# Two recurrent blocks run side by side and earlier, other column orders, and half-width first levels, in a two-model Trainium2 kernel

## The chip, the cores and the metric

The kernel runs on one core of one Trainium2 chip. A core has a matrix engine (TensorE, PE in the profile), a vector engine (VectorE, DVE), an engine for functions such as exp (ScalarE, ACT), a general one (GpSimd, POOL) and one that mostly issues transfers (SyncE, SP). PE writes its results to PSUM, which has 8 banks; everything else lies in SBUF. The metric is the device time of one launch in microseconds, median of several runs.

## The reference, cut to what matters

Two models run after each other: two transformer layers, and then two layers of a hybrid. Each hybrid layer is a *mixer* followed by a feed-forward part. The change touches the mixer alone, which runs twice. T is 528 tokens.

```python
proj = jnp.einsum('btd,dc->btc', h, w_in)
hq, hf, hi, hg, rq, rk, rv, rg, lx, ly = jnp.split(proj, IN_SPLITS, axis=-1)
... # HGRN: 4 heads of width 128, from hf (decay, key), hq (query), hi (value)
o_hg = merge_heads(rmsnorm(o_hg, hg_norm_g)) * jax.nn.silu(hg)
... # retention: 4 heads, from rq, rk (with rope) and rv
o_ret = merge_heads(head_groupnorm(o_ret, ret_norm_g)) * jax.nn.silu(rg)
xc = causal_dwconv(lx, lru_conv_w, lru_conv_b)          # 4 taps, 256 channels
o_lru = rg_lru(xc, gate_a_w, gate_a_b, gate_i_w, gate_i_b, lru_lambda) * jax.nn.gelu(ly)
merged = jnp.concatenate([o_hg, o_ret, o_lru], axis=-1)
return jnp.einsum('btc,cd->btd', merged, w_out)

# rg_lru: r and i are sigmoids of two block-diagonal products of xc
log_a = -LRU_C * r * softplus(-lam);  a = exp(log_a)
u = sqrt(-expm1(2.0 * log_a)) * (i * x);  h_t = a_t h_{t-1} + u_t
```

## The kernel before, in words

**Matrix products.** A weight tile of 128 columns is brought from memory to `raw` by SP, copied to a rounded high part `WH` by ACT (`highs`, L1207) and subtracted to a low part `WL` by DVE (`lows`, L1761). Each product is made of three PE passes (low weights, low activations, both high; `part`, L516). The high part of unit u+3 can be made when PE has finished unit u, so `highs` for it stands in ACT's program right behind the eviction of unit u; DVE's `lows` stands two slots later in its own program. Every engine runs its program strictly in order.

**The mixer.** PE computes the columns of `w_in` tile by tile in the order of `MIXER_TILES`; GH and GL are the high and low part of the merged result, whose 8 blocks (0 to 3 HGRN heads, 4 and 5 retention, 6 and 7 LRU) are read by the output projection in `out_first`. A plain tile has 8 *slots* (one for each of 8 contraction steps, 6 matmuls of 264 columns each), a wide one (`v0`, `v1`, `rv`: values, computed by `wide_tokens`, L604) has 20. Slots are counted through: `lx0` is slots 1 to 8, `lx1` 9 to 16, `v0` 17 to 36, `hf1` 37 to 44, `hq1` 45 to 52, `hg1` 53 to 60, `rq0` 61 to 68, up to slot 196, and the output projection's first two tiles bring slots 197 to 208.

**The woven work.** HGRN's heads, LRU, retention and the two gates are generators, one for each engine. `Threads` advances them: a work `(generator, n, a, b)` makes its step i at slot a + ceil(i (b-a) / n). So head 0 `(14, 1, 52)` makes step 6 at slot 20, 7 at 27 and so on by the same rule on PE, ACT and DVE; the step's work is put into the engine's program behind that slot's. Slots order the programs, they don't synchronise the engines: an engine waits only where an instruction waits on a semaphore. ACT evicts a tile after the steps of that tile's last slot; in the wide tile it evicts bank by bank, the last bank after the steps of the last slot.

**An HGRN head.** Step 1 on DVE makes the decay A (L2209) and the key K (`hK`, L2211) and prepares level 0. Steps 2 to 7 are the levels -1 to 4: PE multiplies 32-column blocks (L967) into bank 4, DVE merges the bank under a mask (`merge`, L2203) and prepares the level after next (`prep`, L2186 to L2199). PE's next level may write bank 4 only after the merge before it. Step 8 is levels 5 and 6, step 9 transposes (L993), step 10 PE makes the chunk states (L1001, L1003, which read the values `VI` of the wide tile) and DVE chains them, step 11 PE makes the head's output (L1019) and ACT squares and copies it (L1543, L1544), step 12 PE sums the squares, ACT makes the inverse root (a table load and `Ln` and `Exp`, L1547 to L1550) and DVE scales (L2251), step 13 DVE gates (L2256) and ACT copies to GH (L1553), step 14 DVE makes GL (L2259).

**LRU, block n of 2.** Each block runs alone, through one set of buffers (`xc`, `la`, `li`, `tmp[3]`), so block 1 begins after block 0's scan. `(lru(), 8, 10, 60)` gives slots 17, 23, 29, 35 for block 0 and 42, 48, 54, 60 for block 1. The four steps: DVE's convolution (L2273, L2276); PE's product for gate a (L523) and ACT's sigmoid (L1564); PE's product for gate i, ACT's sigmoid, tanh and exp (L1567, L1569, L1570), DVE's products (L2281 to L2286); ACT's square root (L1573), DVE's product and scan (L2289, L2291).

**Retention's norm.** At slots 176 and 180 PE makes the means, at 184 and 187 the variances (L523), both into banks 6 and 7; ACT takes `Ln` and `Exp` of each (L1608, L1610).

**The ends.** `lru_gate` (slots 176, 180, 184) multiplies by gelu(ly) and writes blocks 6 and 7; `ret_gate` (194, 200, 206) writes blocks 4 and 5. `out_first` reads the blocks in the order 0, 1, 2, 6, 7, 3 in its first two tiles, and `finish_tile` adds 4 and 5.

Of the kernel before, what the change touches and what calls it, by code (L numbers as in the profile page):

```python
# [8 lines left out]
T = 528  # L9
# [262 lines left out]
def build(nc, wts, xT, mT, pp, cst, cstm, tA, tR, causal, biasT, gates, out, spill):  # L272
# [10 lines left out]
    with ctx:  # L283
# [87 lines left out]
        at = Counts()  # L371
# [127 lines left out]
        def pe_program(nc, e):  # L499
# [531 lines left out]

            def lru(l):
                for n in range(2):
                    yield
                    pe.wait_ge(*at("lconv", l, n))
                    pe.wait_ge(gw_loaded, 16 * (l + 1))
                    take(6, 7)
                    ones_sum(gw[:, n, :], xc, two(3), True, True).then_inc(*pe.up("lga", l, n))
                    give((6, 7), ("lsa", l, n))
                    yield  # L1040
                    take(6, 7)
                    ones_sum(gw[:, 2 + n, :], xc, two(3), True, True).then_inc(*pe.up("lgi", l, n))
                    give((6, 7), ("lsi", l, n))
                    yield
                    yield

# [34 lines left out]
            def ret_values(l):  # L1081
# [36 lines left out]
                for n in range(2):  # L1118
# [17 lines left out]
            def mixer(l, between):  # L1136
# [19 lines left out]
                UO = first[f"mo{l}"]  # L1156
                out_first(UO, works, GH, GL, (0, 1, 2, 6, 7, 3), [pair_of(0, ver), pair_of(1, ver)], ("gl", l), 0)

                def tiles(m, r):
                    if m < 2:  # L1160
                        finish_tile(UO + m, r, GH, GL, (4, 5), ("gl", l), 0)
                    else:
                        tile(UO + m, r, GH, GL)
# [30 lines left out]
        def act_program(nc, e):  # L1194
# [361 lines left out]
            def lru(l):  # L1556
                lbv = lbvs[l]
                for n in range(2):
                    yield
                    act.wait_ge(*at("lga", l, n))  # L1560
                    if n:
                        act.wait_ge(*at("la6", l, 0))
                    act.wait_ge(*at("dk", l, 25))
                    nc.scalar.activation(la, pair_bank(3), ACT.Sigmoid, bias=par("gab", 2 * l + n)).then_inc(*act.up("lsa", l, n))  # L1564
                    yield
                    act.wait_ge(*at("lgi", l, n))
                    nc.scalar.activation(li, pair_bank(3), ACT.Sigmoid, bias=par("gib", 2 * l + n)).then_inc(*act.up("lsi", l, n))  # L1567
                    act.wait_ge(*at("lsa", l, n))
                    nc.scalar.activation(tmp[3], la, ACT.Tanh, scale=lbv[:, 24 + n:25 + n]).then_inc(*act.up("lth", l, n))  # L1569
                    nc.scalar.activation(la, la, ACT.Exp, scale=lbv[:, 26 + n:27 + n]).then_inc(*act.up("lea", l, n))  # L1570
                    yield
                    act.wait_ge(*at("la3", l, n))
                    nc.scalar.activation(tmp[3], tmp[3], ACT.Sqrt).then_inc(*act.up("lsq", l, n))  # L1573
                    yield

# [15 lines left out]
            def ret_values(l):  # L1591
# [12 lines left out]
                for n in range(2):  # L1604
                    act.wait_ge(*at("rvar", l, n))
                    act.wait_ge(*at("hst", l, 3, 3))
                    nc.scalar.preload_act_table_set("natural_log_exp_and_others")
                    nc.scalar.activation(tmp_rs[n][:, :], pair_bank(3), ACT.Ln, bias=eps6).then_inc(*act.up("rl", l, n))  # L1608
# [11 lines left out]
            def mixer(l):  # L1620
# [129 lines left out]
        def dve_program(nc, e):  # L1750
# [416 lines left out]
            def hgrn(l, h):  # L2167
# [3 lines left out]
                def prep(lev):  # L2171
# [11 lines left out]
                    if lev:  # L2183
                        dve.wait_ge(*at("hA", l, h, lev - 1))
                    if lev < 2:
                        nc.vector.tensor_tensor(qa[:, :], Q[:, :], A[:, :], ALU.mult).then_inc(*dve.up("hd1" if lev else "hp", l, h, lev))  # L2186
                    else:
                        nc.vector.tensor_tensor(QAv[:, :, 1, :], Qv[:, :, 1, :], Av[:, :, 1, :], ALU.mult).then_inc(*dve.up("hd1", l, h, lev))
# [73 lines left out]
            def lru(l):  # L2262
                for n in range(2):
                    x = LX[n]
# [6 lines left out]
                    if n:  # L2271
                        dve.wait_ge(*at("la6", l, 0))
                    nc.vector.tensor_scalar(xc, x[:, 3:T + 3], cw(3), par("lcb", 2 * l + n), ALU.mult, ALU.add).then_inc(*dve.up("lc", l, n, 0))  # L2273
                    for j in range(3):
                        dve.wait_ge(*at("lc", l, n, j))
                        nc.vector.scalar_tensor_tensor(xc, x[:, j:j + T], cw(j), xc, ALU.mult, ALU.add  # L2276
                                                       ).then_inc(*dve.up(*(("lc", l, n, j + 1) if j < 2 else ("lconv", l, n))))
                    yield
                    yield
                    dve.wait_ge(*at("lsi", l, n))  # L2280
                    nc.vector.tensor_tensor(xc, xc, li, ALU.mult).then_inc(*dve.up("lix", l, n))  # L2281
                    dve.wait_ge(*at("lea", l, n))
                    dve.wait_ge(*at("lix", l, n))
                    nc.vector.tensor_tensor(li, la, la, ALU.mult).then_inc(*dve.up("la2", l, n))
                    dve.wait_ge(*at("la2", l, n))
                    nc.vector.scalar_tensor_tensor(tmp[3], li, 1.0, tmp[3], ALU.add, ALU.mult).then_inc(*dve.up("la3", l, n))  # L2286
                    yield
                    dve.wait_ge(*at("lsq", l, n))
                    nc.vector.tensor_tensor(xc, xc, tmp[3], ALU.mult).then_inc(*dve.up("la5", l, n))  # L2289
                    dve.wait_ge(*at("la5", l, n))  # L2290
                    nc.vector.tensor_tensor_scan(hseq[n], la, xc, 0.0, ALU.mult, ALU.add).then_inc(*dve.up("la6", l, n))  # L2291
                    yield

# [18 lines left out]
            def ret_scores(l):  # L2312
                for n, r in enumerate((RQ, RK)):
                    dve.wait_ge(*at("rperm", l, n))
                    dve.wait_ge(tab_loaded, 16 * (l + 1))
                    dve.wait_ge(*(at("la6", l, 1) if n else at("lconv", l, 1)))
                    nc.vector.tensor_tensor(rraw[n], rraw[n], tab[:, 2 * n, :], ALU.mult).then_inc(*dve.up("rropec", l, n))
# [278 lines left out]
```

## Time and profile before

| what | value |
|---|---|
| median of 3 runs | 2693.39 us (2691.96 to 2695.31) |
| the profiled execution | 2695.57 us, its span 2693.8 us |
| PE / DVE / ACT busy | 2609.5 / 1367.1 / 1058.2 us (97% / 51% / 39%) |
| first mixer, slots 1 to 196 | 1357.6 to 1578.2 us of the span |
| second mixer, slots 1 to 196 | 2035.7 to 2255.0 us |

Times of the trace are microseconds from the first instruction. In a waits view a row says which engine and line waited for which, then the sum, the number of waits and the longest. In a timeline a row has the start, the duration, engine, line, operation, operands and count, and in brackets the idle time before it with what ended it. `ACT_TABLE_LOAD` is ACT's change from one set of functions to another. In a row of a windows view stand the stretch and its length, the busy time of PE, PE's weight loads, DVE, ACT and POOL with the number of instructions, the granted TensorE clock as a share of full speed (1.00 is the 2.4 GHz level, 0.50 the 1.2 GHz level), the DMA engines' busy share and GB/s.

### The profile page before, as it was taken

Reading aid. Unit: us, or ns where it says so; the run is one execution under the profiler, and the core shown is the slowest. Engines: PE = TensorE matmul, PEld = TensorE weight load, DVE = VectorE, ACT = ScalarE, POOL = GpSimd, SP = SyncE. Lnnn points to the kernel's source line nnn. Section 1 sums busy time; section 2 is a strip of 40 time slices with the busy share of each in tenths; the row PEclk is TensorE's granted clock in tenths of the full one; section 3 lists DMA queues with packets and bytes.
Section 4 is the critical chain, followed back from the end, with each engine's and each line's share of the span. In section 5 each row is a group of like instructions: output and inputs, shape, how many; then the busy total and the mean of one; then the engine's idle time right before and its main releaser. Section 6 shows DMA issues by size and latency. Waiting matters only on the chain.

```text
span 2693.8 us, 42806 instructions
## 1 busy us (share of the span) xinstructions
PE 2609.5 (97%) x18948; PEld 2327.8 (86%) x18948; DVE 1367.1 (51%) x2195; ACT 1058.2 (39%) x1713; POOL 30.6 (1%) x69
## 2 busy tenths in 40 slices
PE   7999999999999999999999999999999999999998
PEld 5776888888877788888798899999999889999998
DVE  4776633324555653332566546555336654655533
ACT  3554422222444442221454344444225444444421
POOL 0000000000000000000000000000000000000000
PEclk9999999999999999999999999999999999999999
DMA  4221122222222122232221222222223122222222
GB/s 164 83 87 62 67 97 98 95 87 90 94 79 79 64 78 94 94 102 88 81 98 48 84 91 79 95 91 80 99 87 123 48 84 80 90 95 94 90 87 75
DMA packets 39467, 236.04 MB, mean 88 GB/s; under 512 B 5248, under 2 KB 7296, under 8 KB 17008
## 3 DMA queue, kind: packets, MB, share of 16 engines
q1 hardware_dynamic: 34336, 213.93, 23.5%
q0 software_dynamic: 3792, 17.26, 1.8%
q8 instruction: 149, 2.44, 0.4%
q10 hardware_dynamic: 1152, 2.10, 0.2%
q14 instruction: 38, 0.31, 0.0%
HBM read 222.65 MB, written 6.42 MB: 85 GB/s over the span
## 4 chain that ended last, share of the span: by engine, by line
PE 85%; DVE 8%; ACT 6%; DMA 1%; issue 0%; ACTq 0%; DVEq 0%
PE P L516 72%; PE P L626 2%; PE P L604 2%; PE P L523 2%; DVE WL L1761 2%; ACT WH L1207 1%; PE P L881 1%; PE P L638 1%; PE P L652 1%; PE P L681 1%; PE P L967 1%; DVE X L2061 1%; DVE small L2064 1%; DMA X<-in_xT 0%; PE P L857 0%
## 5 line engine op out<-in xcount | busy, mean ns | idle before, releaser
L516 PE MATMUL P<-XH,WL 128*128 128x264 f32 (+3 forms) x3080 | 850.2, 325 | 35.0 <-DVE WL L1761 19.4
L516 PE MATMUL P<-XL,WH 128*128 128x264 f32 (+3 forms) x3080 | 825.8, 317 | 0.0
L516 PE MATMUL P<-XH,WH 128*128 128x264 f32 (+3 forms) x3080 | 823.6, 316 | 0.0
L1761 DVE TENSOR_TENSOR WL<-raw,WH 128x1024 fp32r<-128x1024 f32 (+1 forms) x404 | 483.8, 1201 | 552.0 <-ACT WH L1207 551.5
L1207 ACT ACTIVATE WH<-raw 128x1024 fp32r<-128x1024 f32 (+1 forms) x404 | 418.3, 1039 | 598.2 <-PE P L516 597.3
L516 PEld LDWEIGHTS P<-XH,WL 128*128 128x128 f32 x3080 | 522.6, 189 | 83.5 <-issue 19.0
L516 PEld LDWEIGHTS P<-XH,WH 128*128 128x128 f32 x3080 | 521.5, 190 | 38.3
L516 PEld LDWEIGHTS P<-XL,WH 128*128 128x128 f32 x3080 | 521.6, 189 | 35.5
L2416 DVE SCALAR_TENSOR_TENSOR tmp<-P,PP,tmp 128x527 f32<-128x527 f32 (+1 forms) x88 | 66.8, 759 | 195.2 <-ACT tmp L1710 195.2
L516 PE MATMUL P<-GHH,WL 128*128 128x264 f32 (+1 forms) x704 | 149.1, 283 | 0.0
L516 PE MATMUL P<-GHL,WH 128*128 128x264 f32 (+1 forms) x704 | 148.8, 282 | 0.0
L516 PE MATMUL P<-GHH,WH 128*128 128x264 f32 (+1 forms) x704 | 148.7, 282 | 0.0
L516 PE MATMUL P<-HH,WL 128*128 128x512 f32 (+2 forms) x396 | 147.4, 372 | 0.0
L516 PE MATMUL P<-HL,WH 128*128 128x512 f32 (+2 forms) x396 | 146.6, 370 | 0.0
L516 PE MATMUL P<-HH,WH 128*128 128x512 f32 (+2 forms) x396 | 146.6, 370 | 0.0
L1710 ACT ACTIVATE tmp<-P,PP 128x528 f32<-128x528 f32 (+1 forms) x88 | 69.2, 786 | 186.8 <-PE P L516 186.8
L516 PEld LDWEIGHTS P<-GHH,WL 128*128 128x128 f32 x704 | 112.1, 188 | 0.1
L516 PEld LDWEIGHTS P<-GHL,WH 128*128 128x128 f32 x704 | 112.0, 188 | 0.1
L516 PEld LDWEIGHTS P<-GHH,WH 128*128 128x128 f32 x704 | 111.9, 188 | 0.0
L516 PEld LDWEIGHTS P<-HH,WL 128*128 128x128 f32 x396 | 74.5, 188 | 14.2
L516 PEld LDWEIGHTS P<-HL,WH 128*128 128x128 f32 x396 | 74.5, 188 | 14.1
L516 PEld LDWEIGHTS P<-HH,WH 128*128 128x128 f32 x396 | 74.5, 188 | 13.9
(346 smaller groups left out, 3442.6 us busy)
## 6 DMA issues: line engine op xcount, KB each, us to landing
raw<-in_wts SPq DMA_DIRECT2D x170, 1024.0 KB, 4.9
raw<-in_wts SPq DMA_DIRECT2D x32, 896.0 KB, 4.7
spill<-X POOLq DMA_DIRECT2D x2, 2112.0 KB, 8.9
X<-spill POOLq DMA_DIRECT2D x16, 264.0 KB, 3.1
tmp<-in_biasT POOLq DMA_DIRECT2D x16, 256.0 KB, 4.0
qswap<-qraw SPq DMA_DIRECT2D x44, 64.0 KB, 2.0
tab<-in_tR POOLq DMA_DIRECT2D x2, 1056.0 KB, 5.7
X<-in_xT ACTq DMA_DIRECT2D x8, 256.0 KB, 13.2
```

The costliest lines, as they stand in the source:

```text
L516: ins = nc.tensor.matmul(P[:, a:a + x1 - x0], wb[:, s, 128 * k:128 * k + 128], xb[:, kx, x0 - c0:x1 - c0], start=start and i == 0, stop=st ...
L523: ins = nc.tensor.matmul(P[:, a:a + x1 - x0], m, src[:, x0 - c0:x1 - c0], start=start, stop=stop)
L604: ins = nc.tensor.matmul(o, xb[:, k, c0:c1], wb[:, (u + k // 4) % NS, 256 * (k % 4):256 * (k % 4) + 256], start=n == 0 and k == 0 and i == ...
L626: ins = nc.tensor.matmul(o, xb[:, k, c0:c1], wb[:, (u + k // 4) % NS, 256 * (k % 4):256 * (k % 4) + 256], start=n == 0 and k == 0 and i == ...
L638: ins = nc.tensor.transpose(P[:, 512 * b + 128 * j:512 * b + 128 * j + 128], src[:, 128 * j:128 * j + 128], ident)
L652: nc.tensor.matmul(P[:, o:o + ke], q[64 * m:64 * m + 64, lane, 128 * i:128 * i + 128], k[64 * m:64 * m + 64, 2 + lane, 0:ke], start=(j == ...
L681: ins = nc.tensor.matmul(P[:, o + 128 * j:o + 512], VN[:, j, vc:vc + 128], aTs[lane][:, 512 * j:384 * j + 512], start=(j == 0), stop=(j == 3))
L881: ins = nc.tensor.matmul(P[s0:s0 + 64, o:512 * b + 512], VB[:, j, vc + s0:vc + s0 + 64], aTB[lane][hf][:, 512 * j:384 * j + 512], start=(j ...
L1207: nc.scalar.activation(WH[:, u % NS, 0:length(u)], raw[:, u // 2 % RAW, a:a + length(u)], ACT.Copy).then_inc(*act.up("whi", u))
L1710: nc.scalar.activation(y[:, a0:], pair_bank(n % 4)[:, a0:], ACT.Identity, bias=par("fcb", 44 * l + c), scale=PP[:, k:k + 1]).then_inc(*act ...
L1761: nc.vector.tensor_tensor(WL[:, u % NS, 0:length(u)], raw[:, u // 2 % RAW, a:a + length(u)], WH[:, u % NS, 0:length(u)].bitcast(F), ALU.su ...
L2416: nc.vector.scalar_tensor_tensor(y[:, a0 + 1:T], p[:, a0:T - 1], w(1), y[:, a0 + 1:T], ALU.mult, ALU.add).then_inc(*dve.up("conv1", l, n))
```

## The change

Four things change, all in the mixer:

1. **LRU.** The two blocks no longer follow each other through one buffer set; each has its own (`la`, `li`, `lth`, and `hseq` in the place of `xc`), and the steps are at slots 14, 19, 24, 29, 34, 39, 44 and 49. DVE: convolution 0 (14), convolution 1 (19), product with gate i of block 0 (29) and 1 (39), the products L2284 and L2286 of both (44), product and scan of both (49). PE: the four gate products at 19, 24, 29 and 34. ACT: sigmoids at 19, 24, 29, 34, at 34 then tanh of both and exp of both, at 44 the square roots of both.
2. **Tile order and dates.** `hg3`, `rg0` and `rg1` come before `ly0` and `ly1`. `lru_gate` is at slots 196, 202 and 207, `ret_gate` at 189, 194 and 199. Head 2 goes from `(98, 136)` to `(96, 134)`, so its steps 1, 2, 3 and 11 are at 99, 102, 105 and 127; head 3 from `(138, 184)` to `(140, 184)`, so its steps 1 and 2 are at 144 and 147. The output projection's first two tiles read blocks 0 to 5 in order, and `finish_tile` adds 6 and 7.
3. **Retention's variances** go into banks 6 and 7 for n = 0 and banks 4 and 5 for n = 1.
4. **Half-width levels.** For heads 1 to 3, `prep` of level 0 and 1 writes only the half of QA that is read, and that of level 1 and 2 only that half of KB; head 0 still writes them whole.

```diff
-               ("hf2", 8), ("hq2", 8), ("v1", 20), ("hg2", 8), ("hf3", 8), ("hq3", 8), ("rv", 20), ("ly0", 8),
-               ("ly1", 8), ("hg3", 8), ("rg0", 8), ("rg1", 8)]
+               ("hf2", 8), ("hq2", 8), ("v1", 20), ("hg2", 8), ("hf3", 8), ("hq3", 8), ("rv", 20), ("hg3", 8),
+               ("rg0", 8), ("rg1", 8), ("ly0", 8), ("ly1", 8)]
...
-    return Threads((hgrn(0), 14, 1, 52), (hgrn(1), 14, 54, 96), (hgrn(2), 14, 98, 136), (hgrn(3), 14, 138, 184),
-                   (lru(), 8, 10, 60), (ret_scores(), 6, 78, 114), (ret_values(), 8, 157, 187), (lru_gate(), 3, 172, 184),
-                   (ret_gate(), 3, 188, 206))
+    return Threads((hgrn(0), 14, 1, 52), (hgrn(1), 14, 54, 96), (hgrn(2), 14, 96, 134), (hgrn(3), 14, 140, 184),
+                   (lru(), 8, 9, 49), (ret_scores(), 6, 78, 114), (ret_values(), 8, 157, 187), (lru_gate(), 3, 190, 207),
+                   (ret_gate(), 3, 184, 199))
...
-        xc, la, li = (X[:, k, :] for k in (3, 4, 5))
+        la, li = (X[:, 3, :], X[:, 5, :]), (X[:, 4, :], tmp[3])
+        lth = [LX[n][:, 0:T] for n in range(2)]
... (PE)
+                yield
                 for n in range(2):
-                    yield
                     pe.wait_ge(*at("lconv", l, n))
...
-                    ones_sum(gw[:, n, :], xc, two(3), True, True).then_inc(*pe.up("lga", l, n))
+                    ones_sum(gw[:, n, :], hseq[n], two(3), True, True).then_inc(*pe.up("lga", l, n))
...
                 for n in range(2):
+                    p = 3 - n
                     pe.wait_ge(*at("rsq", l, n))
-                    take(6, 7)
-                    ones_sum(ones_ret, rsq[n][:, :], two(3), True, True).then_inc(*pe.up("rvar", l, n))
-                    give((6, 7), ("rl", l, n))
+                    take(2 * p, 2 * p + 1)
+                    ones_sum(ones_ret, rsq[n][:, :], two(p), True, True).then_inc(*pe.up("rvar", l, n))
+                    give((2 * p, 2 * p + 1), ("rl", l, n))
...
-                out_first(UO, works, GH, GL, (0, 1, 2, 6, 7, 3), [pair_of(0, ver), pair_of(1, ver)], ("gl", l), 0)
+                out_first(UO, works, GH, GL, range(6), [pair_of(0, ver), pair_of(1, ver)], ("gl", l), 0)
... (ACT)
+                    nc.scalar.activation(la[n], pair_bank(3), ACT.Sigmoid, bias=par("gab", 2 * l + n)).then_inc(*act.up("lsa", l, n))
                     yield
                     act.wait_ge(*at("lgi", l, n))
+                    nc.scalar.activation(li[n], pair_bank(3), ACT.Sigmoid, bias=par("gib", 2 * l + n)).then_inc(*act.up("lsi", l, n))
+                    if n == 0:
+                        yield
+                for n in range(2):
                     act.wait_ge(*at("lsa", l, n))
+                    act.wait_ge(*at("lconv", l, 1))
+                    nc.scalar.activation(lth[n], la[n], ACT.Tanh, scale=lbv[:, 24 + n:25 + n]).then_inc(*act.up("lth", l, n))
+                for n in range(2):
+                    nc.scalar.activation(la[n], la[n], ACT.Exp, scale=lbv[:, 26 + n:27 + n]).then_inc(*act.up("lea", l, n))
+                yield
+                yield
+                for n in range(2):
                     act.wait_ge(*at("la3", l, n))
+                    nc.scalar.activation(lth[n], lth[n], ACT.Sqrt).then_inc(*act.up("lsq", l, n))
... (DVE)
-                    if lev < 2:
+                    if lev < 2 and h == 0:
                         nc.vector.tensor_tensor(qa[:, :], Q[:, :], A[:, :], ALU.mult).then_inc(*dve.up("hd1" if lev else "hp", l, h, lev))
...
-                    if 0 < lev < 3:
+                    if h == 0 and 0 < lev < 3:
                         nc.vector.tensor_tensor(kb[:, :], K[:, :], B[:, :], ALU.mult).then_inc(*dve.up("hp", l, h, lev))
...
+                conv(0)
+                yield
+                conv(1)
+                yield
+                yield
+                gated(0)
+                yield
+                yield
+                gated(1)
+                yield
+                for n in range(2):
                     dve.wait_ge(*at("lea", l, n))
                     dve.wait_ge(*at("lix", l, n))
+                    nc.vector.tensor_tensor(li[n], la[n], la[n], ALU.mult).then_inc(*dve.up("la2", l, n))
                     dve.wait_ge(*at("la2", l, n))
+                    nc.vector.scalar_tensor_tensor(lth[n], li[n], 1.0, lth[n], ALU.add, ALU.mult).then_inc(*dve.up("la3", l, n))
+                yield
+                for n in range(2):
                     dve.wait_ge(*at("lsq", l, n))
+                    nc.vector.tensor_tensor(hseq[n], hseq[n], lth[n], ALU.mult).then_inc(*dve.up("la5", l, n))
                     dve.wait_ge(*at("la5", l, n))
+                    nc.vector.tensor_tensor_scan(hseq[n], la[n], hseq[n], 0.0, ALU.mult, ALU.add).then_inc(*dve.up("la6", l, n))
+                yield
```

## Rows read from the trace of the kernel before

**Rows 1.** Waits of PE in the first mixer: engine, line, releaser: total us, times, longest

```profile
PE P L967 <- DVE hK L2211: 7.1, 2, 5.7
PE P L991 <- DVE hKB L2234: 0.7, 1, 0.7
```

**Rows 2.** Windows of both mixers and of stretches in them

```profile
1357.60:1578.20 220.60, 208.04 (x2414) 192.36 (x2415) 130.40 (x245) 108.35 (x157) 5.85 (x11) 0.98 0.21 69
2035.70:2255.00 219.30, 206.89 (x2413) 191.06 (x2414) 128.81 (x243) 107.76 (x156) 5.85 (x11) 0.98 0.20 68
...
1419.90:1426.80 6.90, 3.88 (x49) 3.85 (x50) 6.59 (x13) 4.26 (x5) 0.00 (x0) 0.51 0.46 153
...
1570.00:1573.60 3.60, 3.60 (x19) 3.60 (x18) 0.29 (x1) 3.43 (x4) 0.00 (x0) 0.53 0.28 75
2244.80:2252.00 7.20, 4.61 (x35) 4.48 (x35) 3.18 (x4) 6.46 (x8) 0.54 (x1) 1.00 0.15 40
```

**Rows 3.** Timeline of PE in the first mixer, slots 20, 23, 38 and 187

```profile
1374.18 0.46 PE L967 MATMUL P<-hQA,hKB 128*32 128x32 f32 x32
...
1377.96 0.43 PE L967 MATMUL P<-hQA,hKB 128*32 128x32 f32 x29 [0.98 <-DVE SD L2203]
...
1394.35 0.45 PE L1001 MATMUL P<-VI,KT 16*128 16x128 f32 x2 [0.37 <-ACT VI L1675]
...
1565.83 0.28 PE L516 MATMUL P<-XL,WH 128*128 128x264 f32 x1
1565.95 0.41 PE L516 MATMUL P<-XH,WH 128*128 128x264 f32 x2
1568.96 1.13 PE L523 MATMUL P<-hQ,C 128*128 128x264 f32 x4 [2.60 <-ACT hB L1608]
```

**Rows 4.** Timeline of DVE, head 0's levels and the first convolution

```profile
1369.76 0.43 DVE L2188 TENSOR_TENSOR hQA<-hQ,hA 128x264 f32<-128x264 f32 x1
...
1371.66 0.32 DVE L2203 COPY_PREDICATED SD<-masks,P 128x144 f32<-128x144 uint8 x1
...
1373.49 0.55 DVE L2273 TENSOR_SCALAR X<-X,PP 128x528 f32<-128x528 f32 x1
...
1376.37 1.22 DVE L1761 TENSOR_TENSOR WL<-raw,WH 128x1024 fp32r<-128x1024 f32 x1
```

**Rows 5.** Timeline of ACT, LRU's functions and the wide tile's last eviction

```profile
1385.07 0.70 ACT L1567 ACTIVATE X<-P,PP 128x528 f32<-128x528 f32 x1 [1.20 <-PE P L523]
1385.67 0.73 ACT L1569 ACTIVATE tmp<-X,lbv 128x528 f32<-128x528 f32 x1
1386.41 1.28 ACT L1570 ACT_TABLE_LOAD   x1
1387.71 0.74 ACT L1570 ACTIVATE X<-X,lbv 128x528 f32<-128x528 f32 x1
...
1393.62 0.58 ACT L1675 ACTIVATE VI<-P 128x512 f32<-128x512 f32 x1
1394.10 1.05 ACT L1207 ACTIVATE WH<-raw 128x1024 fp32r<-128x1024 f32 x1
```

**Rows 6.** Timeline of ACT, head 0's square and the Exp of its norm

```profile
1401.39 0.62 ACT L1543 ACTIVATE tmp<-P 128x528 f32<-128x528 f32 x1 [5.29 <-PE P L1019]
...
1407.93 0.65 ACT L1550 ACTIVATE tmp<-tmp 128x528 f32<-128x528 f32 x1
```

**Rows 7.** Timeline of DVE from head 0's scaling to LRU's last scan

```profile
1408.61 0.77 DVE L2251 SCALAR_TENSOR_TENSOR tmp<-hQA,PP,tmp 128x528 f32<-128x528 f32 x1 [6.32 <-ACT tmp L1550]
...
1422.37 0.49 DVE L2211 TENSOR_SCALAR hK<-tmp,lbv 128x528 f32<-128x528 f32 x1
...
1426.94 0.70 DVE L2289 TENSOR_TENSOR X<-X,tmp 128x528 f32<-128x528 f32 x1
1427.68 1.26 DVE L2291 TENSOR_TENSOR_SCAN X<-X 128x528 f32<-128x528 f32 x1
```

**Rows 8.** Timeline of ACT, retention's second square

```profile
1562.11 0.65 ACT L1602 ACTIVATE hQ<-hKB 128x528 f32<-128x528 f32 x1 [1.45 <-DVE hKB L2352]
```

More of the change, by code:

```diff
@@ L1041, in lru @@
                     take(6, 7)
-                    ones_sum(gw[:, 2 + n, :], xc, two(3), True, True).then_inc(*pe.up("lgi", l, n))
+                    ones_sum(gw[:, 2 + n, :], hseq[n], two(3), True, True).then_inc(*pe.up("lgi", l, n))
                     give((6, 7), ("lsi", l, n))
                     yield
-                    yield
+                yield
+                yield
+                yield
             def ret_scores(l):
@@ L1156, in mixer @@
                 UO = first[f"mo{l}"]
-                out_first(UO, works, GH, GL, (0, 1, 2, 6, 7, 3), [pair_of(0, ver), pair_of(1, ver)], ("gl", l), 0)
+                out_first(UO, works, GH, GL, range(6), [pair_of(0, ver), pair_of(1, ver)], ("gl", l), 0)
                 def tiles(m, r):
                     if m < 2:
-                        finish_tile(UO + m, r, GH, GL, (4, 5), ("gl", l), 0)
+                        finish_tile(UO + m, r, GH, GL, (6, 7), ("gl", l), 0)
                     else:
@@ L1607, in ret_values @@
                     nc.scalar.preload_act_table_set("natural_log_exp_and_others")
-                    nc.scalar.activation(tmp_rs[n][:, :], pair_bank(3), ACT.Ln, bias=eps6).then_inc(*act.up("rl", l, n))
+                    nc.scalar.activation(tmp_rs[n][:, :], pair_bank(3 - n), ACT.Ln, bias=eps6).then_inc(*act.up("rl", l, n))
                     act.wait_ge(*at("rl", l, n))
@@ L1650, in evict @@
                         act.wait_ge(*at("unit", u))
-                        act.wait_ge(*at("lconv", l, n))
+                        act.wait_ge(*at("la5", l, 1))
                         nc.scalar.activation(rraw[n], pair_bank(p), ACT.Copy).then_inc(*act.up(name, l, n))
@@ L2184, in prep @@
                         dve.wait_ge(*at("hA", l, h, lev - 1))
-                    if lev < 2:
+                    if lev < 2 and h == 0:
                         nc.vector.tensor_tensor(qa[:, :], Q[:, :], A[:, :], ALU.mult).then_inc(*dve.up("hd1" if lev else "hp", l, h, lev))
                     else:
-                        nc.vector.tensor_tensor(QAv[:, :, 1, :], Qv[:, :, 1, :], Av[:, :, 1, :], ALU.mult).then_inc(*dve.up("hd1", l, h, lev))
-                    if 0 < lev < 3:
+                        nc.vector.tensor_tensor(QAv[:, :, 1, :], Qv[:, :, 1, :], Av[:, :, 1, :], ALU.mult
+                                                ).then_inc(*dve.up("hd1" if lev else "hp", l, h, lev))
+                    if h == 0 and 0 < lev < 3:
                         nc.vector.tensor_tensor(kb[:, :], K[:, :], B[:, :], ALU.mult).then_inc(*dve.up("hp", l, h, lev))
@@ L2262, in lru, with conv @@
             def lru(l):
-                for n in range(2):
-                    x = LX[n]
+                def conv(n):
+                    x, y = LX[n], hseq[n]
                     def cw(j):
@@ L2270, in lru @@
                     dve.wait_ge(*at("lx", l, n))
-                    if n:
-                        dve.wait_ge(*at("la6", l, 0))
-                    nc.vector.tensor_scalar(xc, x[:, 3:T + 3], cw(3), par("lcb", 2 * l + n), ALU.mult, ALU.add).then_inc(*dve.up("lc", l, n, 0))
+                    nc.vector.tensor_scalar(y, x[:, 3:T + 3], cw(3), par("lcb", 2 * l + n), ALU.mult, ALU.add).then_inc(*dve.up("lc", l, n, 0))
                     for j in range(3):
                         dve.wait_ge(*at("lc", l, n, j))
-                        nc.vector.scalar_tensor_tensor(xc, x[:, j:j + T], cw(j), xc, ALU.mult, ALU.add
+                        nc.vector.scalar_tensor_tensor(y, x[:, j:j + T], cw(j), y, ALU.mult, ALU.add
@@ L2277, in lru, with gated @@
                                                        ).then_inc(*dve.up(*(("lc", l, n, j + 1) if j < 2 else ("lconv", l, n))))
-                    yield
-                    yield
+                def gated(n):
                     dve.wait_ge(*at("lsi", l, n))
-                    nc.vector.tensor_tensor(xc, xc, li, ALU.mult).then_inc(*dve.up("lix", l, n))
+                    nc.vector.tensor_tensor(hseq[n], hseq[n], li[n], ALU.mult).then_inc(*dve.up("lix", l, n))
+                conv(0)
@@ L2282, in lru @@
+                yield
+                conv(1)
+                yield
+                yield
+                gated(0)
+                yield
+                yield
+                gated(1)
+                yield
+                for n in range(2):
                     dve.wait_ge(*at("lea", l, n))
                     dve.wait_ge(*at("lix", l, n))
-                    nc.vector.tensor_tensor(li, la, la, ALU.mult).then_inc(*dve.up("la2", l, n))
+                    nc.vector.tensor_tensor(li[n], la[n], la[n], ALU.mult).then_inc(*dve.up("la2", l, n))
@@ L2290, in lru @@
                     dve.wait_ge(*at("la5", l, n))
-                    nc.vector.tensor_tensor_scan(hseq[n], la, xc, 0.0, ALU.mult, ALU.add).then_inc(*dve.up("la6", l, n))
-                    yield
+                    nc.vector.tensor_tensor_scan(hseq[n], la[n], hseq[n], 0.0, ALU.mult, ALU.add).then_inc(*dve.up("la6", l, n))
+                yield
             def lru_gate(l):
@@ L2315, in ret_scores @@
                     dve.wait_ge(tab_loaded, 16 * (l + 1))
-                    dve.wait_ge(*(at("la6", l, 1) if n else at("lconv", l, 1)))
+                    dve.wait_ge(*at("la6", l, 1))
                     nc.vector.tensor_tensor(rraw[n], rraw[n], tab[:, 2 * n, :], ALU.mult).then_inc(*dve.up("rropec", l, n))
```

14 lines of the change are left out of this document (1 added, 13 removed).

## The prediction

> **What bounds the kernel now.** I read the busy times first, where PE stands far ahead of every other engine, and then the windows of the two mixers, since the change touches nothing else. In the first mixer PE is busy 208.04 of 220.60 us, in the second 206.89 of 219.30 [rows 2]: 12.5 us of pauses in each, and the rest is matmul work that the change neither adds to nor takes from. So the change can act in two ways alone: on these pauses, and on the granted clock, which fell to the 1.2 GHz level behind the longer of them (0.51 over 6.90 us and 0.53 over 3.60 us) but not behind the second mixer's last one (1.00 over 7.20 us) [rows 2]. The waits say what the pauses are: head keys that DVE makes late, 7.1 us in two waits with 5.7 the longest, and the transposes' operand at slot 34, 0.7 [rows 1]. In PE's timeline stand 0.98 at slot 23, 0.37 at slot 38 and 2.60 before retention's second variance, which waits for an ACT Ln [rows 3]. That leaves 0.7 us in two small ones of retention and levels. The second mixer repeats them, so I work one mixer out and double it.
>
> I follow each engine's program in its new order, with durations from the rows. What a step adds to its engine is the distance of two starts, which is shorter than an operation's length by up to 0.1 us. Two matmuls of 264 columns start 0.12 us apart [rows 3], so a slot is 6 x 0.12 = 0.73 us; a gate product or variance (four fp32 matmuls, 1.13 us to its last end [rows 3]) delays PE by 0.9.
>
> **LRU, first convolution.** DVE is free for it at 1371.66, where the merge of head 0's step 4 stands [rows 4]. It takes 1376.37 - 1373.49 = 2.9 [rows 4], to 1374.6. PE comes to the gate product at slot 19, one slot before 1374.18 [rows 3], at 1373.5: **a new pause of 1.2 us** with 0.1 of signalling.
>
> **Second convolution.** DVE goes on with step 4 (1373.49 - 1371.66 = 1.8), a low part (1.14) and the convolution (2.9), and so comes to the merge of step 5 at 1380.4, done at 1380.7. PE leaves slot 19 at 1374.8, does the product (0.9), one level (0.6) and four slots (2.8) and stands at slot 23 at 1379.1, where level 3 may not write bank 4 before that merge: **1.7 us**, in the place of 0.98 [rows 3].
>
> **Tanh and exp of both blocks.** PE's place at slot 38 was 1394.35 - 0.37 = 1394.0 [rows 3]. It is now later by the new pauses (2.9), without the old ones (0.98 and 0.7), and by two gate products that come sooner (1.8): 1396.9. At slot 34 ACT has the second gate product at about 1394.0 and then, in its program, sigmoid (0.60), two tanh (2 x 0.65), the load of exp's functions (1.30) and two exps (2 x 0.65) [rows 5], and only then the wide tile's last eviction (0.58 [rows 5]): 1399.1. PE's chunk states at slot 38 read these values: **2.5 us** in the place of 0.37.
>
> The Trainium skill's page "ScalarE: Activation LUTs", section "Table sets: the hidden batching unit", asks for exactly this, all calls of one set together, and its section "What ACT_TABLE_LOAD costs" counts 2.66 us for a change of set, of which 1.38 is a drain. The trace disagrees on the drain: 1386.41 to 1387.71 is 1.30 us from the load's start to the exp's [rows 5]. By the page's figure the pause at slot 38 would be an estimated 1.4 us longer; the measurement decides. The loads saved (7 in LRU, 3 after) are on an engine that is not the bound.
>
> **The key of head 1.** This is the 5.73 us wait [rows 1], and it ought to go, since LRU's last DVE step moves from slot 60 to slot 49. But another chain feeds it. ACT squares head 0's output at 1401.39 and ends its Exp at 1408.58, 7.2 us later [rows 6], and DVE, which waits for that Exp at 1408.61 after 6.32 us of idleness [rows 7], has all that follows queued behind. Now the square starts later by the pauses (1.2 + 1.7 + 2.5 against 0.98 + 0.7 + 0.37, so 3.35) and the two gate products (1.8): 1406.5. Between it and the Exp stand LRU's load (1.3) and two square roots (2 x 0.65), 2.6 more: 1406.5 + 7.2 + 2.6 = 1416.3. Behind it on DVE: scaling 0.7, low part 1.14, gating 0.6, product and scan of both blocks 2 x 1.9 (1426.94 to 1427.68 and 1.2 for the scan [rows 7]), GL 0.6, low part 1.14, A and K 0.95 (K's length 0.49 [rows 7]): 9.0 us, K at 1425.3. PE is at slot 60 at 1422.9 - 5.73 = 1417.2 (K's end was 1422.86 [rows 7]), plus 3.35: 1420.5, since by then both orders have all four gate products. **4.8 us** in the place of 5.73. This is the place where I chose: everyone would take the moved dates for the cure, I take the chain through ACT.
>
> **Heads 2 and 3.** Head 2's step 2 now shares slot 102 with retention's scores, which need bank 4: PE waits for the merge just asked for, about **0.6 us**, new. Head 3's first level comes two slots (1.4 us) later while its key doesn't, so the other 1.4 us of the key waits [rows 1] is gone. The 0.5 us at retention's first mean stays.
>
> **Half-width levels.** An operation takes 0.43 instead of 0.70 [rows 4, 7], four of them in each of three heads: 3.2 us of DVE time a mixer. No pause stands behind one of them; nothing. At most it takes 0.3 from the wait at slot 102; if DVE's work on head 1 were a bound, it would give up to 1.1.
>
> **Variances.** The second no longer waits for the first one's Ln: 2.6 us gone, and PE is through slot 196 at (1568.96 - 2.60) + 0.9 + 9 x 0.73 = 1573.8 [rows 3].
>
> **The projection's order.** ACT, though, has the same to do. From the second square at 1562.11 [rows 8]: square 0.65, load 1.3, eviction rg1 0.5, high part 0.95, GH3 0.65, two times load, Ln and Exp at 2.7, load 1.3, gelu 0.5, high part 1.05: 1574.5. Then DVE: low part 1.14, gating 0.6, GL4 0.6 (block 4 at 1577.0), gelu product 0.7: 1577.6. ACT: GH6 0.55, eviction ly1 0.5, high part 1.05 [rows 5]: 1579.7. DVE: low part 1.14 and GL5 0.7: 1581.6. PE asks for block 4 at 1573.8 + 4 x 0.73 = 1576.7 and waits **0.3**, and for block 5 at 1577.8 and waits **3.9**. Before, blocks 4 and 5 were needed 12 slots behind. Blocks 6 and 7 are ready by 1584, before PE wants them.
>
> **Clock.** The fall behind the 5.7 us wait covers 6.9 us with 3.9 of PE work [rows 2], which loses half of it, 1.9, or 1.7 by the distances of the slots; the one behind the 2.6 us wait the same. That is 2 x 1.7 + 1.8 = 5.2 in both mixers. I count 1.7 behind each pause of 4.8 and 3.9, and 2.5 for both mixers together behind the two of 2.5, since 2.6 us once brought a fall and once not: 9.3. Nothing for 1.2 and 1.7, where bounds are 0 and 3.4.
>
> **Sum.** New pauses 1.2 + 1.7 + 2.5 + 4.8 + 0.6 + 0.5 + 4.2 = 15.5 against 12.5: +3.0 a mixer, +6.0; clock +4.1; together +10.1. From the profiled execution's 2695.57 that is 2705.7. It lies 2.2 above the median, so 2693.4 + 10.1 = **2703.5 us**. Each pause is a difference of two chains of some ten terms; I allow 0.8 on each of the four large ones, so 3 to 6 in all, and 3.5 on the clock.
>
> **Rivals.** *A, the dates cure it.* If DVE gets head 0's Exp early enough that K is ready at slot 60, and block 5 is ready in time, the mixer loses 5.7 + 1.7, 1.4 and 2.6 + 0.9 and gains 0.9 + 0.6, so -10.8: 2 x that gives 2672. For it: LRU's products stand right before K now. Against it: the 6.32 us of idleness before the scaling [rows 7], which shows DVE waiting for ACT, not for LRU. The Trainium skill's grouping rule, cited above, speaks for it.
> *B, only the end is right.* The pause at the projection vanishes, the rest as forecast: -3.9 - 1.7 twice, 2692, no change. It holds if ACT finds its Exps 4 us sooner; the work between is all in its program, so I doubt it.
> *C, more clock.* Pauses of 1.2 and 1.7 within 6 us of each other bring a fall as well, and the one at slot 38 brings it in both mixers: +3.4 and +0.9, 2708. This one is on the forecast's side; the mechanism that decides against the forecast is A's, from the point at which ACT's Exp is ready 4.8 us sooner than I have it.
> *D, the change doesn't do what it says.* LRU does end by slot 49 in the programs, but not in time: in my working its last scan ends at 1422.5, behind slot 60. That is part of the forecast.
>
> **How the numbers follow.** Forecast with C 0.70, A or a good part of it 0.16, B 0.14. A measurement tells about 0.2% (5.4 us) from no change, so slower means above 2698.8: 0.70; same 0.14; faster 0.16. The range from 2690 to 2711 holds B and the forecast with its errors and C, and leaves A out. The forecast's own range is 2697 to 2710.
>
> **What would show it.** In the changed profile: PE's waits list LRU's convolution (about 1.2), the merge (1.7), the values (2.5), hK (4.8, once a mixer) and a wait of the output projection on GL (3.9), and no wait on Ln; the clock is low behind the last three. Right before K, DVE idles before L2251 for ACT's Exp. I am wrong if the hK wait is under 2 us or the projection doesn't wait.

## The result, and the profile after

The changed kernel takes 2703.19 us (median of 6 runs, 2702.86 to 2709.08), the one before beside it 2692.68 (2691.48 to 2695.31): a ratio of 1.0041, 95% interval 1.0031 to 1.0051, so 8 to 14 us slower. The forecast was 2703.5. Its profiled execution took 2706.04 us with a span of 2704.2.

PE's waits in the first mixer of the changed kernel, where [rows 1] had 7.1 us on hK; the columns are engine and line, releaser, total us, times, longest:

```profile
PE P L968 <- DVE hK L2222: 4.7, 1, 4.7
PE P L517 <- DVE GL L2394: 3.8, 2, 3.6
PE P L1002 <- ACT VI L1685: 2.4, 1, 2.4
PE P L968 <- DVE SD L2214: 1.6, 1, 1.6
PE P L524 <- DVE X L2285: 1.2, 1, 1.2
PE P L1063 <- DVE SD L2214: 0.7, 1, 0.7
PE P L524 <- ACT hQA L1548: 0.5, 1, 0.5
PE P L980 <- DVE hKB L2203: 0.3, 1, 0.3
```

The wait on Ln (2.6) is gone, the longest on hK is shorter by 1.0, and the second one on hK (head 3's, 1.4) and the transposes' 0.7 are gone. But four large ones stand there that [rows 3] did not show or showed smaller: the values (VI, 2.4 for 0.37), the merge (SD, 1.6 for 0.98), LRU's convolution (X, 1.2) and, the largest of the new ones, block 5 of the projection (GL, 3.6). Together 15.1 us for 12.5.

The windows of the changed kernel, slots 1 to 196 of both mixers and then the stretches of low clock in them and in the projections behind them, with the columns of [rows 2]:

```profile
1359.20:1577.10 217.90, 206.50 (x2414) 190.99 (x2415) 123.41 (x240) 97.73 (x148) 4.77 (x9) 0.98 0.20 67
2040.40:2259.90 219.50, 208.09 (x2414) 192.55 (x2415) 123.40 (x240) 97.70 (x148) 4.77 (x9) 0.98 0.19 66
...
2082.80:2086.20 3.40, 3.40 (x18) 3.40 (x17) 2.22 (x5) 1.03 (x2) 0.00 (x0) 0.50 0.02 5
1424.00:1430.90 6.90, 4.31 (x51) 4.27 (x52) 6.63 (x13) 1.12 (x2) 0.00 (x0) 0.51 0.45 153
2106.70:2113.50 6.80, 4.14 (x50) 4.11 (x51) 6.53 (x13) 1.18 (x2) 0.00 (x0) 0.50 0.44 154
1584.40:1587.90 3.50, 3.04 (x14) 3.04 (x15) 2.35 (x4) 1.93 (x2) 1.08 (x2) 0.51 0.14 25
2267.10:2270.60 3.50, 2.93 (x13) 2.94 (x14) 2.46 (x4) 1.94 (x2) 1.08 (x2) 0.51 0.12 17
```

Note what the first row would mislead one to: the stretch up to slot 196 is 2.7 us *shorter* than in [rows 2], since the longest new pause lies behind slot 196, in the projection. In these rows DVE is 7 us less busy than in [rows 2] and ACT 11, but part of that is work that the change moved behind slot 196; over the whole execution, with both mixers, DVE went from 1367.1 to 1360.2 us and ACT from 1058.2 to 1041.3. Both have less to do and the kernel is slower: neither was the bound.

The clock fell in five places of the two mixers with their projections, three before. Both profiles side by side put the second mixer's start at 2035.7 and 2040.4 and the ends of the spans at 2693.8 and 2704.2. Of these 10.4 us, 1.6 arose ahead of the first mixer (it begins at 1359.2 for 1357.6), where nothing was changed: the low clock that begins at 215 us lasts 3.6 us in one profile and 6.8 in the other. 3.1 come from the stretch of the first mixer and what follows up to the second, and 5.7 from the second to the end; the second mixer alone has two more clock falls. So this one execution shows 8.8 us of the change's own.

### The profile page after: what moved, and what is told of

Read it like the earlier page. It is cut to its first block, busy times and chain, and to the rows that moved or that the text cites. A ratio compares the mean times of both kernels' runs of the same rounds, so it can differ in the third digit from the quotient of the medians.

```text
span 2704.2 us, 42776 instructions
## 1 busy us (share of the span) xinstructions
PE 2614.3 (97%) x18948; PEld 2331.6 (86%) x18948; DVE 1360.2 (50%) x2195; ACT 1041.3 (39%) x1701; POOL 30.6 (1%) x69
## 4 chain that ended last, share of the span: by engine, by line
PE 85%; DVE 9%; ACT 5%; DMA 1%; issue 0%; ACTq 0%; DVEq 0%
PE P L517 72%; PE P L627 2%; PE P L605 2%; DVE WL L1771 2%; PE P L524 2%; ACT WH L1211 1%; PE P L882 1%; PE P L639 1%; PE P L653 1%; PE P L682 1%; PE P L968 1%; DVE X L2071 1%; DVE small L2074 1%; DMA X<-in_xT 0%; PE P L858 0%
```

## The experiments

Each kernel was timed beside the one before in the same series; times are medians, ratios have their 95% interval. Times of two kernels of different series are compared by their ratios to the kernel before, and such a difference is uncertain by 0.13 to 0.20% (4 to 5 us). The executions of one kernel spread by 1 to 10 us, and the profiles show where much of that may come from: the same pauses bring a low clock in one execution and none in another.

**The LRU part alone, and all but the LRU.**

```diff
# e1: the kernel before
-                   (lru(), 8, 10, 60), ...
+                   (lru(), 8, 9, 49), ...      # with the changed lru() on PE, ACT and DVE
# e2: the changed kernel
-                   (lru(), 8, 9, 49), ...
+                   (lru(), 8, 10, 60), ...     # with the lru() of before
```

> The kernel before with the new LRU alone (both blocks together, steps at slots 14 to 49); tile order, heads' dates, variances and whole-width levels as before. Theory (ACT's functions and DVE's convolutions stand in PE's way, and the key of head 1 comes late through head 0's Exp): per mixer pauses of about 1.2 at slot 19, 1.6 at slot 23, 2.4 at slot 38 and 4.7 on hK, 9.9 in the place of 7.8, so +4 us in both mixers and 0 to 2 of clock: 4 to 6 us above the kernel before. Rival (ending LRU by slot 49 frees DVE for the key): the 5.7 us wait and the low clock behind it go, and the kernel is 10 to 15 us below the one before.

> The changed kernel with the LRU of the kernel before (slots 17 to 60, one buffer set). Theory: head 0's pauses are those of before (0.98, 0.7, 0.37, 5.7 on hK), the wait on Ln and the second wait on hK are gone, 0.7 at slot 102 and 3.8 before block 5 come in: pauses +0.6 per mixer, and the end's clock fall in both mixers, together 2 to 4 us above the kernel before. Rival (the LRU is all that costs, the rest of the change is a gain): 4 to 8 us below the kernel before.

The LRU alone: 2699.61 us for 2694.21, ratio 1.0023 [1.0014, 1.0032]. All but the LRU: 2698.06, ratio 1.0015 [1.0007, 1.0024]. Each half of the change is slower by itself, and 1.0023 and 1.0015 add to 1.0038 for the whole's 1.0041. PE's waits of e1, first mixer:

```profile
PE P L968 <- DVE hK L2220: 6.1, 2, 4.7
PE P L524 <- ACT hB L1617: 2.6, 1, 2.6
PE P L1002 <- ACT VI L1684: 2.4, 1, 2.4
PE P L968 <- DVE SD L2212: 1.6, 1, 1.6
PE P L524 <- DVE X L2283: 1.2, 1, 1.2
```

These are the changed kernel's pauses of 1.2, 1.6, 2.4 and 4.7, so the LRU alone brings them. Head 3's wait on hK (the other 1.4 of the 6.1) and the one on Ln are still there. In PE's waits of e2, first mixer, hK is back at 5.7, head 3's wait is gone, and the 3.6 us before block 5 stay:

```profile
PE P L967 <- DVE hK L2213: 5.7, 1, 5.7
PE P L516 <- DVE GL L2374: 3.8, 2, 3.6
```

Both rivals, which had one half as a gain, are out.

**Square roots behind head 0's Exp.** ACT's step 7 of the LRU at slot 46 for 44:

```diff
-                   (lru(), 8, 9, 49), ...
+                   # on ACT alone: steps at 14, 19, 24, 29, 34, 39, 46, 49
```

> The changed kernel, but ACT takes LRU's two square roots (with their load of functions, 2.6 us together) at slot 46, behind head 0's Ln and Exp, instead of slot 44 ahead of them. Nothing else moves. Theory (K waits for a chain through that Exp): Exp and with it K come 2.6 us sooner, the hK wait falls from 4.7 to about 2.1, 5 us and up to 3 of clock: 5 to 8 us below the changed kernel. Rival (the queue of LRU's products and scans on DVE is what holds K, and it waits for the square roots): the hK wait stays at 4.7 or grows, no gain.

2699.67 us, ratio to before 1.0020 [1.0010, 1.0029]. PE's wait on hK in the first mixer of e3 is now

```profile
PE P L971 <- DVE hK L2225: 2.1, 1, 2.1
```

2.6 us shorter, by what the root's load and two roots took, and 2.2 in the second mixer. DVE's queue behind the Exp is the same as in the changed kernel and isn't held by the later roots, so K is set by the chain through the Exp, of which that queue is the last 9 us. In time, 1.0020 against the changed kernel's 1.0041 is 0.21%, 5.7 us, where 5 to 8 were expected, but uncertain by 4. The profiled execution shows no gain by the clock: the shorter pause still brought a low clock in both mixers, and its low stretches there are six with 27.3 us together, for five with 24.1 in the changed kernel. It is one of the slowest of e3's ten, 2703.47 us at a mean granted clock of 0.992; the three at 0.995 took 2695.4 to 2696.6.

**GL5 ahead of the low part.**

```diff
-                   ... (lru_gate(), 3, 190, 207),
-                   (ret_gate(), 3, 184, 199))
+                   ... (lru_gate(), 3, 196, 208),
+                   (ret_gate(), 3, 184, 198))
```

> The changed kernel with lru_gate at slots 200, 204 and 208 instead of 196, 202, 207 and ret_gate's last step at 198 instead of 199, so that GL5 stands ahead of DVE's low part and ly1's eviction doesn't wait for the gelu product of block 6. Theory (block 5 is late only because of what is queued ahead of it): the pause of 3.8 us before block 5 and the low clock behind it go, 9 to 11 us below the changed kernel, about the kernel before. Rival (retention itself is late, its Ln and Exp): the pause stays above 3 us, no gain.

2691.91 us, ratio 0.9997 [0.9988, 1.0006]: the whole loss of the change is gone by moving the dates of two works, with the tile order and the projection's order as in the changed kernel. Among PE's waits of e4 in the first mixer the one on GL fell from 3.8 to

```profile
PE P L517 <- DVE GL L2394: 0.2, 1, 0.2
```

and no fall of the clock follows it. Retention was ready; what was late was what I had found queued ahead of GL5. How much of it is GL5's own date and how much the later `lru_gate`, no run separates.

**The values first.**

```diff
-                    if n == 0:
-                        yield
+                    yield          # tanh and exp one step later, at slot 39
...
-                yield
```

> The changed kernel, but ACT takes LRU's tanh and exp of both blocks at slot 39, behind the wide tile's last eviction, instead of slot 34 ahead of it. Theory (PE's chunk states at slot 38 wait only for that eviction): the pause of 2.4 us at slot 38 goes in both mixers, and the low clock that sometimes follows it; the hK wait stays at 4.7, since head 0's square and slot 60 come sooner by the same 2.4: 5 to 7 us below the changed kernel. Rival (tanh and exp are only moved into the chain to head 0's Exp): the hK wait grows by what slot 38 loses, no gain.

2697.69 us, ratio 1.0018 [1.0009, 1.0027]. The wait on VI isn't in the list of PE's waits of e5 (first mixer) any more, and those on hK and GL stay:

```profile
PE P L968 <- DVE hK L2220: 4.7, 1, 4.7
PE P L517 <- DVE GL L2392: 3.6, 1, 3.6
```

So the 2.4 us were the eviction's place in ACT's program and weren't passed on. Against the changed kernel that is 0.23%, 6.2 us, as forecast.

**The three together.**

> The changed kernel with the three edits together: square roots behind head 0's Exp, tanh and exp behind the eviction, GL5 ahead of the low part. Theory (three causes, each with its own chain): pauses of 1.2, 1.6, 2.1, 0.7, 0.3, 0.5 and 0.2 remain, 6.5 in the place of 15.1 per mixer, 17 us and 4 to 6 of clock: 21 to 23 us below the changed kernel, 11 to 13 below the one before. Rival (the chains run into each other): less than 15 us.

2679.51 us, ratio 0.9949 [0.9936, 0.9961]; pauses of 1.2, 1.6, 2.2, 0.7, 0.3 and 0.5 us remain, 6.4 in the first mixer and 6.6 in the second, and the clock doesn't fall in either in the profiled execution, the fastest of the five. The median is 13.8 us below the kernel before, where 11 to 13 were forecast.

**Whole-width levels.** The condition `h == 0` taken out of `prep`:

> The changed kernel with whole-width levels 0 to 2 in all heads. Theory (no pause stands behind these operations): DVE 6.5 us busier, pauses and time as in the changed kernel, within 0.2%; at most 0.3 us more at slot 102. Rival (the half widths pay in heads 1 to 3 and hide part of the loss): 2 to 6 us above the changed kernel.

2703.72 us, ratio 1.0043 [1.0031, 1.0056], the changed kernel's own within the interval; DVE is 5.8 us busier. PE's waits in the first mixer differ from the changed kernel's by 0.2 us at most, and in one place where DVE's levels are waited for:

```profile
PE P L1063 <- DVE SD L2214: 0.9, 1, 0.9
```

0.9 for 0.7 at slot 102, the one place where a merge is waited for right behind a level's start. By the waits the half widths are worth that and no more; the times alone would allow some 4 us either way.

**Dates worked out from the chains.** `e8` has LRU dates for each engine, head 2 at its old dates, and the two edits for GL5 and the values:

```diff
+ PE  14, 21, 24, 29, 34, 39, 41, 43      # gate products at 21, 24, 29, 34
+ ACT 14, 21, 24, 29, 34, 39, 41, 43      # tanh, exp at 39, roots at 41
+ DVE 14, 24, 24, 29, 34, 39, 40, 43      # convolutions at 14, 24; scans at 43
```

> The changed kernel with GL5 ahead of the low part, head 2 back at its old dates, and LRU at dates worked out from the chains: DVE convolutions at slots 14 and 24, products with gate i at 29 and 34, the other products at 39 and 40, scans at 43; PE's gate products at 21, 24, 29, 34; ACT's sigmoids there, tanh and exp at 39, square roots at 41, ahead of head 0's square. Theory: no pause at slots 19, 23, 38, 60 and 102 over 0.3 us, since K no longer has scans (3.8) or square roots (2.6) ahead of it; about 1.2 of pauses per mixer in the place of 15.1 and no low clock in the mixers: 32 to 37 us below the changed kernel, near 2668. Rival (something else holds K, such as head 0's own norm): a wait on hK of 2 us or more stays, 2680 or above.

2676.71 us, ratio 0.9940 [0.9928, 0.9953]: faster, but my expectation failed by 9 us, and the rival's condition held, a wait on hK of 2.6 with a low clock behind it in both mixers (its time, 2680 or above, did not). DVE's timeline of e8 (start in us, duration, line, operation, and in brackets the idle time before it with what ended it) shows that it is not head 0's norm:

```profile
1411.22 0.77 DVE L2263 SCALAR_TENSOR_TENSOR tmp<-hQA,PP,tmp 128x528 f32<-128x528 f32 x1 [3.97 <-ACT tmp L1557]
...
1414.45 0.71 DVE L2271 TENSOR_TENSOR GL<-tmp,GH 128x528 fp32r<-128x528 f32 x1 [0.71 <-ACT GH L1560]
1417.32 1.23 DVE L1772 TENSOR_TENSOR WL<-raw,WH 128x1024 fp32r<-128x1024 f32 x1 [2.16 <-ACT WH L1214]
1418.46 0.55 DVE L2221 TENSOR_SCALAR hA<-tmp,lbv 128x528 f32<-128x528 f32 x1
1418.93 0.49 DVE L2223 TENSOR_SCALAR hK<-tmp,lbv 128x528 f32<-128x528 f32 x1
```

With scans and roots out of the way DVE idles 2.16 us before a *low part*, whose high part ACT makes only behind GH0, a load of functions and the eviction of hq1. K stands behind that low part though it needs nothing of it. In my working of the changed kernel the low part had always been ready in time, and I had taken its place for granted. The 0.7 us at slot 20 is the convolution put ahead of a merge, a thing of the same kind.

**Two dates more.**

```diff
-(hgrn(1), 14, 54, 96)
+(hgrn(1), 14, (54, 60, 63, 66, 69, 72, 75, 78, 81, 84, 87, 90, 93, 96), 0)
-DVE 14, 24, 24, 29, 34, 39, 40, 43
+DVE 17, 24, 24, 29, 34, 39, 40, 43
```

> The kernel of e8_new_dates with two dates moved: head 1's step 1 (A and K on DVE) at slot 54 instead of 57, which puts it ahead of the low part that waits for ACT's eviction of hq1 and the high part behind it; and the first convolution at slot 17 instead of 14, behind the merge of head 0's step 4. Theory (in e8 K waited 2.6 us only because of that low part, and slot 20 waited 0.7 us only because of the convolution ahead of the merge): both pauses go, head 0's norm is early enough; 1.2 of pauses remain per mixer, 7 us and 0 to 3 of clock below e8: 2667 to 2671. Rival (K is held by head 0's norm and GL, which are ahead of it anyway): the hK wait stays over 1.5 us, 2674 or above.

**2667.47 us, ratio 0.9901 [0.9886, 0.9916]**: 27 us below the kernel before, as forecast, and the fastest kernel here. In DVE's timeline of e9 the order is K first, low part later:

```profile
1411.44 0.55 DVE L2221 TENSOR_SCALAR hA<-tmp,lbv 128x528 f32<-128x528 f32 x1
1411.91 0.49 DVE L2223 TENSOR_SCALAR hK<-tmp,lbv 128x528 f32<-128x528 f32 x1
1412.80 0.44 DVE L2199 TENSOR_TENSOR hQA<-hQ,hA 128x264 f32<-128x264 f32 x1 [0.40 <-ACT hQ L1645]
...
1414.10 1.22 DVE L1772 TENSOR_TENSOR WL<-raw,WH 128x1024 fp32r<-128x1024 f32 x1
```

and by the windows of both mixers of e9 they run through at full clock (1.00), with PE idle for 1.9 and 2.0 us of 207.0:

```profile
1354.00:1561.00 207.00, 205.08 (x2413) 189.39 (x2414) 123.41 (x240) 97.72 (x148) 4.75 (x9) 1.00 0.20 70
2019.10:2226.10 207.00, 205.01 (x2414) 189.30 (x2415) 123.44 (x240) 97.72 (x148) 4.75 (x9) 1.00 0.20 70
```

One forecast in it was off: the first convolution back at slot 17 brought a pause of 0.9 us at the gate product of slot 21, which I had left out.

**The variances' banks alone.**

```diff
-                    take(6, 7)
-                    ones_sum(ones_ret, rsq[n][:, :], two(3), True, True)...
+                    take(2 * p, 2 * p + 1)          # p = 3 - n
+                    ones_sum(ones_ret, rsq[n][:, :], two(p), True, True)...
... (ACT)
-                    nc.scalar.activation(tmp_rs[n][:, :], pair_bank(3), ACT.Ln, bias=eps6)...
+                    nc.scalar.activation(tmp_rs[n][:, :], pair_bank(3 - n), ACT.Ln, bias=eps6)...
```

> The kernel before with the variances' banks alone changed (n = 1 into banks 4 and 5). Theory: the 2.6 us wait on Ln goes in both mixers, and since blocks 4 and 5 are read 12 slots into the projection no pause comes in its place: 5 to 7 us below the kernel before, in the changed kernel hidden by the order of the projection. Rival (ACT's Ln and Exp only move the wait to the projection, whatever its order): a pause before block 4 or 5 of 2 us or more, no gain.

2686.72 us, ratio 0.9972 [0.9961, 0.9983]. The wait on Ln is gone from PE's waits of e10 (first mixer); in its place stands only

```profile
PE P L516 <- ACT rstd L1659: 0.4, 1, 0.4
```

before the projection. This part of the change pays, 8.1 us (by the interval 5 to 10), more than the 5 to 7 forecast. All but the LRU (e2) has it too and is 3.9 us slower than the kernel before, so the other parts of e2, tile order, projection order and dates, cost some 12 us together. The projection's order isn't the loss by itself: e4 keeps it and has no wait on GL above 0.2 us. It took away the 12 slots of room behind which late dates did no harm. The one other gain in the waits is head 3's 1.4 us, gone in e2 and there in e1; no run times it alone.

## Why the prediction was right

Against the terms of its sum, for the first mixer; "changed" is the profiled execution of the changed kernel:

| step | forecast | changed | tested by |
|---|---|---|---|
| first convolution, slot 19 | 1.2 | 1.2 | e1 |
| second convolution, slot 23 | 1.7 | 1.6 | e1 |
| tanh and exp before the values, slot 38 | 2.5 | 2.4 | e5: gone |
| key of head 1, slot 60 | 4.8 | 4.7 | e3: 2.1 |
| scores of retention, slot 102 | 0.6 | 0.7 | e7: 0.9; e8, head 2 at its old dates: gone |
| retention's mean | 0.5 | 0.5 | |
| projection, blocks 4 and 5 | 0.3 + 3.9 | 0.2 + 3.6 | e4: 0.2 |
| not foreseen, slot 118 (L980) | 0 | 0.3 | |
| sum | 15.5 | 15.1 | |

**The key of head 1.** The chain can be read in the changed kernel's timelines, first ACT's, then DVE's:

```profile
1407.90 0.61 ACT L1547 ACTIVATE tmp<-P 128x528 f32<-128x528 f32 x1 [5.26 <-PE P L1020]
1408.40 0.61 ACT L1548 ACTIVATE hQA<-P 128x528 f32<-128x528 f32 x1
1409.03 1.28 ACT L1582 ACT_TABLE_LOAD   x1
1410.33 1.18 ACT L1582 ACTIVATE X<-X 128x528 f32<-128x528 f32 x2
1411.53 1.28 ACT L1637 ACT_TABLE_LOAD   x1
...
1416.93 0.65 ACT L1554 ACTIVATE tmp<-tmp 128x528 f32<-128x528 f32 x1
```

```profile
1417.61 0.77 DVE L2262 SCALAR_TENSOR_TENSOR tmp<-hQA,PP,tmp 128x528 f32<-128x528 f32 x1 [8.31 <-ACT tmp L1554]
...
1422.67 1.26 DVE L2313 TENSOR_TENSOR_SCAN X<-X 128x528 f32<-128x528 f32 x1
...
1426.05 0.49 DVE L2222 TENSOR_SCALAR hK<-tmp,lbv 128x528 f32<-128x528 f32 x1
```

Square to Exp 9.7 us (forecast 7.2 + 2.6), Exp to K's end 9.0 (9.0). DVE idles 8.31 us before it gets to the LRU's last scans, where [rows 7] had 6.32. As rival D said of itself, the last scan ends at 1423.9, 2 us behind slot 60 (PE's 1426.59 less the wait of 4.69 is 1421.9). That is 5.0 us sooner than the 1428.9 of [rows 7], with the scans now ahead of K in DVE's program instead of behind it, and K pays for them. Rival A needed that Exp 4.8 us sooner; no run has that alone, and e3, with 2.6, had 2.6 us less of the wait. The price of rival A (2672) was also too good: it left out most of what the pauses at slots 19, 23 and 38 add, which an earlier Exp doesn't touch.

**The projection.** From ACT's second square to GL5 the forecast had 19.5 us; ACT's and DVE's rows are

```profile
1565.38 0.65 ACT L1612 ACTIVATE hQ<-hKB 128x528 f32<-128x528 f32 x1 [1.45 <-DVE hKB L2374]
```

```profile
1582.96 1.23 DVE L1771 TENSOR_TENSOR WL<-raw,WH 128x1024 fp32r<-128x1024 f32 x1 [2.15 <-ACT WH L1211]
1584.10 0.70 DVE L2394 TENSOR_TENSOR GL<-hKB,GH 128x528 fp32r<-128x528 f32 x1
```

with GL5's end at 1584.8, 19.4 us. The low part waits 2.15 us for ACT and holds GL5, which needs nothing of it. Rival B is out with the 3.6 us wait, and e4 (0.2 us of the wait left, 0.9997) shows that this place alone was enough to part no change from slower.

**The clock.** Forecast 9.3 us in both mixers; the rows above have five falls, two of 6.9 and 6.8 us with 4.3 and 4.1 us of PE work in them and three of 3.4 to 3.5 us with 3.4, 3.0 and 2.9. Half of the work in each, an estimate of what the clock cost as the prediction had it, is 2.2, 2.1, 1.7, 1.5 and 1.5, together 8.9. The fall behind slot 38 came in the second mixer alone, which is what 2.5 for both mixers stood for. It could have gone either way: in the five profiles with this pause of 2.4 the clock fell behind it in both mixers twice (e1, e3), in neither twice (e4, e7).

**Half widths and grouping.** Nothing for the half widths was right (e7). The table loads saved brought nothing in time either: with the LRU alone (e1) ACT is 15.4 us less busy and the kernel 5.4 us slower, and the roots' one load, put where it is, is part of what delays the Exp. The Trainium skill's rule of the page "ScalarE: Activation LUTs", section "Table sets: the hidden batching unit", which favoured rival A, holds for ACT's busy time; the row of 1409.03 followed by 1410.33 again shows 1.30 us for a change of set, without the drain of 1.38 us that the page's section "What ACT_TABLE_LOAD costs" counts.

**What was only partly right.** At slot 38 the working's own times, 1399.1 less 1396.9, give 2.2 us and not the 2.5 that it counted; 2.4 was measured. The profiled execution has 1.6 us that are not the change's. The total of 10.5 us agrees with 10.1 better than an interval of 8 to 14 us warrants; that part is luck. The pauses agree one by one, to 0.3 us.

## What to carry to other kernels

Where each engine runs a program in fixed order, a date in the program is not a time: before moving work earlier, find what the first instruction behind it waits for, and follow that chain through the other engines; here DVE idled 6.3 us in front of work that the change moved "sooner". Ask of each instruction ahead of a critical one whether it is needed by it: a weight prepared ahead (here a low part) that is ready too late holds everything queued behind it. Two moves ahead of such low parts, GL5's (e4, 11 us) and K's (e8 to e9, 9 us, each with another date moved), make some 20 of the 36 us between the changed kernel and the fastest. Test the parts of a change one by one: one part here was worth 8 us, and the others spent more than that.

## What the runs showed of the hardware

The granted clock answers to pauses of about the same length in different ways. Counted over the profiled executions, with both mixers of each: behind the pauses of 5.7 us on hK it fell to about 0.5 in 6 of 6, behind those of 4.7 in 10 of 10, behind the 3.6 us before block 5 in 10 of 10, behind the 2.6 us on hK of e8 in 2 of 2, behind the 2.6 us on Ln in 1 of 4 (before, e1), behind the 2.4 us before the values in 5 of 10, behind 2.1 and 2.2 us on hK in 2 of 2 in e3 and in 0 of 2 in e6, and never behind the 1.2 and 1.6 us that stand 6 us apart. So the length of a pause alone doesn't decide it here.

The time of an execution goes with its mean granted clock. Of 58 executions of the kernel before, in three series, the 13 at 0.996 have a median of 2691.1 us, the 12 at 0.995 2693.1, the 28 at 0.994 2695.1 and the 5 at 0.993 2696.6. e9, without a long pause in its mixers, was at 0.998 or 0.999 in all four and spread by 1.1 us.
